# The chain steps between the two token halves of a block turn, in a two-block transformer kernel

## The reference

```python
def second_block(x, ...):
    u = _rms(h, norm1_w[l]) * (1.0 + scale1) + shift1
    proj = u @ w_in[l]
    qa, ka, va, qkv_b, z_b, b_b, a_b, gate_a, gate_b = jnp.split(proj, IN_OFFSETS, axis=-1)
    o_a = _stick_breaking(qa, ka, va)          # 16 heads of 128
    qkv_b = silu(_causal_depthwise_conv(qkv_b, conv_w[l]))
    o_b = _gated_delta_rule(qb, kb, vb, g, beta)   # 16 heads of 128
    ...
def _gated_delta_rule(q, k, v, g, beta):
    m = eye + where(stril, beta * kk * decay, 0.0)   # unit lower triangular
    w_v = solve(beta * v); w_k = solve(beta * exp(gc) * k)
    ...
```

## Time and profile before

| | us |
|---|---|
| median of 3 runs | 2765.46 |
| lowest and highest | 2764.84, 2765.63 |
| the profiled execution | 2769.82 |
| its span | 2768.0 |
| PE busy | 2737.5 |
| DVE busy | 2013.2 |
| ACT busy | 1423.3 |

### The profile page before, as it was taken

How to read it: one execution, slowest core, us unless ns; L and a number is a source line. 1 busy time by engine, 2 the same in 40 slices (tenths; PEclk the granted TensorE clock), 3 DMA queues, 4 the chain that set the end, 5 groups by cost and what they waited for, 6 DMA issues and landing times.

```text
span 2768.0 us, 41524 instructions
## 1 busy us (share of the span) xinstructions
PE 2737.5 (99%) x15778; PEld 2350.9 (85%) x15778; DVE 2013.2 (73%) x3486; ACT 1423.3 (51%) x2426; POOL 280.9 (10%) x734
## 2 busy tenths in 40 slices
PE   7999999999999999999999999999999999999999
PEld 4678888888888888888888888888888888888888
DVE  3468877888986787877778777878978755555554
ACT  3365544555566656566565644445454443444443
POOL 0013410000001122222222221000000000000000
PEclk9999999999999999999999999999999999999999
DMA  9957777878856555555555567888758765566564
GB/s 341 349 176 227 229 247 258 281 275 279 301 182 232 171 182 176 186 181 174 187 174 180 183 207 271 297 294 282 271 175 291 254 186 188 192 191 190 186 196 142
DMA packets 179991, 621.75 MB, mean 225 GB/s; under 512 B 20288, under 2 KB 28752, under 8 KB 179152
## 3 DMA queue, kind: packets, MB, share of 16 engines
q1 hardware_dynamic: 169776, 605.62, 65.6%
q10 hardware_dynamic: 10016, 13.47, 1.5%
HBM read 612.70 MB, written 4.21 MB: 223 GB/s over the span
## 4 chain that ended last, share of the span: by engine, by line
PE 95%; DVE 2%; DMA 2%; ACT 1%; issue 1%; SPq 0%; ACTq 0%; DVEq 0%
PE ps L101 93%; PE ps L104 1%; DMA raw<-in_w_s 1%; DVE wlo L116 1%; DMA xc<-in_xc 0%; DMA q_sw<-q_g 0%; DVE acc L122 0%; ACT whi L107 0%; DVE c_y L122 0%; SPq L134 0%; ACT sb_l L107 0%; ACTq L134 0%; DVE d_t L122 0%; ACT L110 0%; ACT k_y L107 0%
## 5 line engine op out<-in xcount | busy, mean ns | idle before, releaser
L101 PE MATMUL ps<-act,whi 128*128 128x512 f32 x5536 | 1356.8, 392 | 0.5 <-DVE act L116 0.5
L101 PEld LDWEIGHTS ps<-act,whi 128*128 128x128 f32 x5536 | 1008.0, 188 | 198.9 <-issue 7.4
L116 DVE TENSOR_TENSOR wlo<-raw,whi 128x1024 fp32r<-128x1024 f32 (+3 forms) x883 | 1039.5, 1186 | 42.5 <-PE ps L101 22.7
L107 ACT ACTIVATE whi<-raw 128x1024 fp32r<-128x1024 f32 (+3 forms) x883 | 894.9, 1026 | 228.1 <-PE ps L101 144.2
L101 PE MATMUL ps<-act,wlo 128*128 128x256 f32 (+2 forms) x5392 | 779.1, 290 | 0.2 <-DVE wlo L116 0.2
L101 PEld LDWEIGHTS ps<-act,wlo 128*128 128x128 f32 (+1 forms) x5392 | 706.8, 191 | 35.6 <-issue 8.0
L101 PE MATMUL ps<-whi,act 128*128 128x512 f32 x1024 | 286.4, 401 | 0.4 <-DVE x_p L116 0.4
L122 DVE SCALAR_TENSOR_TENSOR acc<-raw,c_act,acc 128x1024 f32<-128x1024 f32 x210 | 268.3, 1278 | 0.0
L101 PEld LDWEIGHTS ps<-whi,act 128*128 128x128 f32 x1024 | 183.4, 188 | 34.7 <-DVE x_p L116 2.1
L101 PE MATMUL ps<-wlo,act 128*128 128x512 f32 x512 | 158.1, 390 | 0.0
L119 POOL TENSOR_SCALAR small<-small 128x2 f32<-128x2 f32 (+3 forms) x236 | 96.2, 408 | 596.0 <-DVE small L119 474.2
(11 more groups left out here) (329 smaller groups left out, 2334.8 us busy)
## 6 DMA issues: line engine op xcount, KB each, us to landing
raw<-in_w_turns SPq DMA_DIRECT2D x754, 512.0 KB, 4.2
raw<-in_w_mods SPq DMA_DIRECT2D x224, 512.0 KB, 4.4
raw<-in_w_s SPq DMA_DIRECT2D x64, 512.0 KB, 7.1
raw<-in_w_turns SPq DMA_DIRECT2D x64, 448.0 KB, 4.4
raw<-in_w_turns SPq DMA_DIRECT2D x32, 384.0 KB, 3.7
raw<-in_w_turns SPq DMA_DIRECT2D x17, 256.0 KB, 3.3
raw<-in_w_kv SPq DMA_DIRECT2D x7, 512.0 KB, 3.7
xc<-in_xc SPq DMA_DIRECT2D x3, 1024.0 KB, 9.7
```

The costliest lines, as they stand in the source:

```text
L101: return self.e.matmul(*args, **more)
L107: return self.e.activation(*args, **more)
L116: return self.e.tensor_tensor(*args)
```

## The change

In a block turn half 1 of the turn before is issued after the chain steps of this turn, where it was issued before them. Half 0 of this turn stays first. Nothing is added or removed; the first turn of a group (no half is held back there) and what follows its last turn have the same order as before. Of a group's turns F0 to F7 (half 0), S0 to S7 (half 1) and chain steps C0 to C7 PE's order was F0 C0 F1 S0 C1 F2 S1 C2 ... F7 S6 C7 S7; it is now F0 C0 F1 C1 S0 F2 C2 S1 ... F7 C7 S6 S7. The programs of DVE, ACT, POOL and SP stay as they are.

```diff
@@ -727,9 +727,6 @@
                 e.wait_ge(*on("hi", n))
             elif turn.block:
                 tokens(turn, 0)
-                if behind:
-                    tokens(behind, 1)
-                behind = turn
             elif turn.low_first:
                 low(turn, False)
             else:
@@ -1001,6 +998,9 @@
             if turn.narrow:
                 continue
             if turn.block:
+                if behind:
+                    tokens(behind, 1)
+                behind = turn
                 continue
             p = high(turn, True) if turn.low_first else low(turn, True)
             p.then_inc(*tell("pe_gemm", "w_done", n))
```

## The result

The changed kernel took 2780.45 us (median of 4 runs, 2779.91 to 2781.12), before 2765.55 us (4 runs): a ratio of 1.0051, 95% interval 1.0039 to 1.0064, 14.9 us slower by the medians (which alone would give a ratio of 1.0054, still inside the interval). The forecast was 2777.9 us, +12.4.

The account below looks back on a forecast made before the run. PE bounds the kernel, busy 2737.5 of 2768.0 us. Losses at `p_m` or `i_x` in 12 blocks sum to 12.4 us, added to the median 2765.46: 2777.9 us, own range 2774.5 to 2780.5, wider range 2769 to 2783.

Parts of the forecast that it names:

- The order on PE and the place where the cover shrinks: Block turns on PE: between C0 and C1 one half product lies instead of two, once in each block.
- The size of a half product, 1.38 us, and the 0.05 us from `p_m` to `g_b`: In a block, C1 comes 1.38 us sooner; its loss is 1.38 minus (spare minus 0.05).
- DVE's schedule holds up to `p_m`: Turn 0 on DVE: nothing ahead of `p_m` waits for a moved step, so its time after `g_a` stays, 2.2 us in head 3.
- The largest lateness in a group counts, not the sum: Within one block losses don't add; head 5 loses 0.87 and head 9 1.37, both at `i_x`.
- Nothing for the later `w_done`: Operands freed by S come some 0.4 us later, plus the wait in turn 1; cost taken as 0.
- The rule on LDWEIGHTS: LDWEIGHTS is 85% busy; its free 15%, 0.2 us per block, could swallow lateness, making about 10 us; not adopted.
- The clock falls: Rival: lower clock behind the longer PE waits; given 0 us of its own, no chance stated.
- the wait for `x_p` ahead of S0: S0 claims the bank `gv` left; this 0.4 us wait was to go, since S0 comes later.
- DVE catches up: Rival: DVE has less queued, so the next block's `p_m` comes 0.5 us sooner; +6.4 us, 2771.9 us, chance 0.12.
- Every block pays whole: Rival: late S0 holds back `w_done`, `wlo` and DVE, so all 12 blocks lose 1.38; +16.6 us, 2782, chance 0.08.
- The two by which the time would have stayed or fallen: Rivals: losses fall in time PE loses anyway, 2765.5 us, chance 0.08; or PE's waits go, 2762 us, chance 0.04.
- the waits vanish: Rival: DVE's place at `p_m` moves earlier with the results, so PE's waits go; −3.4 us, 2762, chance 0.04.

Follow-up runs that it names:

- e1: The new order in turn 1 of every group alone, otherwise the kernel before: 2779.84 us, ratio 1.0050 to before.
- e2: The new order in turns 5 to 7 of every group alone, otherwise the kernel before: 2765.62 us, ratio 0.9996 to before.
- e3: The new order in turns 2 to 7 of every group, otherwise the kernel before: 2773.24 us, ratio 1.0025 to before.
- e6: The changed kernel with level 3's `p_m` and `i_x` put first in their turns on DVE: 2761.80 us, ratio 0.9989 to before.
- e7: The kernel before (old PE order) with level 3's `p_m` and `i_x` put first in their turns on DVE: 2760.34 us, ratio 0.9982.
- e9: The changed kernel with 12 unread products filling PE's wait in head 0's group: 2778.40 us, ratio 1.0045 to before.
- e8: The new order in all groups but that of head 0, which keeps the order before: 2778.80 us, ratio 1.0047 to before.
- e12: A repeat of e7, run beside e11 on the same chip: 2761.07 us, ratio 0.9982 to before.
- e11: The kernel before (old PE order) with `p_m` and `i_x` of all six levels first in their DVE turns: 2780.40 us, ratio 1.0048.

## Why the prediction was right, step by step

- *The order on PE and the place where the cover shrinks* (between C0 and C1, once in each group): right. e1 has the loss with turn 1 alone, e2 has none.
- *The size of a half product, 1.38 us, and the 0.05 us from `p_m` to `g_b`*: right; heads 1, 2, 6, 9 and 10 lose 1.32 to 1.35.
- *DVE's schedule holds up to `p_m`*: right; its distance from `g_a` is 4.89, 4.42, 3.88, 2.22 us for heads 0 to 3, and was 4.89, 4.41, 3.87, 2.23.
- *The largest lateness in a group counts, not the sum*: right, heads 5 and 9, where `i_x` decided; e1 leaves 0.29 and 0.74 of their 0.95 and 1.32. In e3, where `p_m` has its two half products again, the spares at `i_x` give 7.6 us for 7.1 worked out the same way.
- *Nothing for the later `w_done`*: right (e2, e6). The waits that it brought to DVE are not on the path; what the new order costs beside the late steps is the 1.5 us between e6 and e7, and whether `w_done` has a part in that wasn't followed.
- *The rule on LDWEIGHTS*: the sum with it was 10 us, without it 12.4; the groups without the clock come to 12.7 in this profile (15.3 less 2.57). No lateness was swallowed. The Trainium skill's page "Perfetto Trace Analysis" (Identifying the Most-Contended Engine) says that matmul busy time is no good measure of how close TensorE is to its limit, and names LDWEIGHTS busy, beside the share of peak FLOPs, in its place. No run here measures that distance, so the page is neither borne out nor contradicted. It doesn't say which way the matmul time errs, nor that the rest of LDWEIGHTS' time can take up lateness; both were my own steps.
- *"The clock falls ... I give it nothing of its own"*: this failed, and it is the 2.6 us between forecast and result (2.57 us by the profile). I had argued from a wait of 1.41 us that kept 1.00; the wait came to 3.45. The trace of before held a nearer row that I didn't use: the wait of 1.96 us at 200 us with 0.50 behind it. The wait was also longer than my 2.8: 0.4 of the 0.65 us are the wait for `x_p` ahead of S0, which I had let go and which this row of before shows; with S0 behind C1 the same time passes in the wait for `p_m`. The other 0.25 us I can't trace to a row.

```profile
922.46 1.20 PE L101 MATMUL ps<-whi,act 128*128 128x512 f32 x4 [0.39 <-DVE x_p L116]
```

- *The range*: 2780.45 lies at the upper edge of the forecast's own range (2774.5 to 2780.5). The range wasn't worked out from the clock, so that it held with the clock missing from the sum was partly luck.

The rival "DVE catches up" gave 2771.9; that DVE's distances stayed within 0.06 us rules it out. "Every block pays whole" gave 2782 and lay nearer to the result than the forecast (1.6 us off, against 2.6), but by the wrong groups: heads 3, 4, 8 and 11 lost 0.40 to 0.72, not 1.38. The two by which the time would have stayed or fallen are ruled out by the interval; of the one on DVE's place, "the waits vanish", e6 shows what it takes: the steps had to be moved on DVE by hand.

## What to carry to other kernels

When work is reordered on the engine that sets the time, count for each pair of dependent steps how much of that engine's own work lies between them now; where it shrinks, subtract it from the spare in the trace, step by step, and take the largest lateness of each stretch. An engine at 79% busy can still be late at every such place, because it comes to the step in program order: the cure was to put two small steps first in its turn, not to reorder the busy engine; and only these two, as the same for all levels cost 19 us. A wait on TensorE that the change makes longer needs a price for the clock beside its own length: look through the whole trace of before, not only the part that changes, for waits of like length and for the granted clock behind them.

## What the runs showed of the hardware

Behind a wait of 3.45 us of PE the granted clock stood at 0.50 to 0.51 for over 5 us in three profiles and at 0.74 over the same stretch in a fourth, with 1.3 to 2.9 us lost. Twelve products that nobody read, put into the wait, kept it at 1.00. A wait of 2.3 us had full clock behind it in three profiles of the new order and 0.70 to 0.72 in the two others that have it, those in which the wait 50 us earlier had been filled or was short. Shorter waits went either way too: behind those of 1.96, 1.99 and 2.00 us at 200 us (before, e9, e8) the clock was 0.50 over some 3.3 us, behind one of 1.76 us it was so in one profile of 14 (e12, 1.7 us lost), and behind the waits of 1.7 us in the groups no group lost more than its half product. In e11 a wait of 2.5 us had 0.76 behind it and one of 2.7 us, some 35 us later, full clock. How the chip comes to the one or the other behind the same wait isn't shown.
